# Leaving out the dummy matmuls at the norm borders of a four-layer transformer kernel on one NeuronCore

## The chip, the cores and the metric

The kernel runs on one NeuronCore of a Trainium2 chip. The metric is the device time of one execution in microseconds (us). The kernel before takes 1987.98 us, the median of three runs (1987.39 to 1991.22).

TensorE (PE) does the matmuls, VectorE (DVE), ScalarE (ACT) and GpSimd (POOL) the element-wise work; SyncE (SP) issues most DMAs. PE's rows in the trace are of two kinds, PE for the matmul itself and PEld for the load of its stationary operand.

## The reference

Two blocks in a row on x of 512 tokens by 1024 features, in float32. The first has two layers (an HGRN2 and stick-breaking mixer, then an mLSTM mixer, each followed by a convolutional gated feed-forward net), the second has one (dilated and sparse attention, then a gated feed-forward net). Every mixer and every feed-forward net is fed by the same kind of step, an RMS norm with a gain and a shift that come from a conditioning vector:

```python
def rmsnorm(x, g):
    xf = x.astype(jnp.float32)
    y = xf * lax.rsqrt(jnp.mean(xf * xf, axis=-1, keepdims=True) + EPS)
    return y * g.astype(jnp.float32)

def modulate(x, g, shift, scale):
    return (rmsnorm(x, g) * (1.0 + scale) + shift).astype(x.dtype)
...
        h = modulate(x, norm_mix_g[layer], sh_m, sc_m)
        ...
        x = x + (g_m * y).astype(x.dtype)
        h = modulate(x, norm_ffn_g[layer], sh_f, sc_f)
        x = x + (g_f * conv_glu_ffn(h, ffn_w_in[layer], ffn_conv_w[layer], ffn_conv_b[layer],
                                    ffn_w_out[layer])).astype(x.dtype)
```

The output projection of one stage must be finished before the mean square over the features is known, and that must be known before the first matmul of the next projection.

## The kernel before

Features lie on the partitions, tokens along the free axis, so the residual stream x is 8 tiles (KT) of 128 by 512. Weights are streamed from memory by SP in chunks of 128 x 1024 (`w_raw`); POOL splits each chunk into a high and a low part (`w_hi`, `w_lo`), once PE has let go of the buffers, and each product is three matmuls, high by high, high by low, low by high (L447 to L449 in `three`; L474 to L476 where the tokens are the stationary side). Results go to four banks called `gemm`. A projection chunk is 24 such matmuls.

The order on each engine is the order in which its program is written; engines meet at semaphores. There is no scheduler.

A **norm border** is the place between the last projection of a stage and the first of the next. There are six, numbered r: 1 (`even_out` to `ffn0`), 2 (`down0` to `odd_in`), 3 (`odd_out` to `ffn1`), 4 (`down1` to `idx_in`), 5 (`attn_out` to `ffn2`), 6 (`down2` to the final norm and the output). At a border the engines do in turn:

1. PE sums the squares of the first seven tiles over the features, which DVE has collected in `sq_acc`: four one-column matmuls (L536, `partial_sums` in `norm_scale`).
2. DVE adds the last projection tile to `x_res`, ACT squares it (`sq_tile`, L1724), and PE adds that to the sum (L536 again). At border 4 two norms come in a row, and PE sums 8 more for the second (`work`).
3. ACT takes the root (`rms`, L1729 or L2046), DVE the reciprocal (`rstd`, L1114; at border 4 further small steps down to L1147).
4. PE spreads `rstd` over all partitions, with four matmuls against the identity matrix (L558, `bcast`).
5. DVE scales (L1151), ACT shifts and rounds to the high part (`h_hi`, L1738), DVE subtracts for the low part (`h_lo`, L1158), tile by tile; PE starts the next projection with the first tile (`first_tiles`, which takes two output tiles at a time and waits at each of the eight k for `h_lo`).

Between these steps PE is given matmuls whose result nobody reads. They go to bank `M[0]` and are issued by one helper:

```python
            def keep_warm(n):

                for _ in range(n):
                    pe.matmul(M[0][:, 0:256], const("ones"), cst[:, 0:256], start=True, stop=True)
```

With `WARM = (2, 4, 4, 14)` each of borders 1, 2, 3 and 5 has 2 of them between steps 1 and 2, 1 after step 2 and 4 after step 4; border 4 has 2, 3 and 4; border 6 has 2, 1 and none. Four more stand after the first norm at the start of the kernel. That is 4 + 4 x 7 + 9 + 3 = 44. The 14 at the very start (`WARM[3]`) are a loop of their own.

A float32 matmul shows as two instructions in the trace, so one dummy is two records of 128 x 256 on L531, and a spread of four matmuls is eight records on L558.

Of the kernel before, what the change touches and what calls it, by code (L numbers as in the profile page):

```python
# [73 lines left out]
    _g = tuple(a + b for a, b in zip(_g, _u))  # L74
ADA_EARLY = 16
ADA_SLOTS = 4
WARM = (2, 4, 4, 14)

DOWN = (8, 8, 6)

# [90 lines left out]
def build(nc, x_in, wstream, adastream, c_in, cols_in, const_in, mask_in, gatew_in, wuk_in, wuv_in, out):  # L171
    with ExitStack() as ctx:
# [3 lines left out]
        def sb(name, shape, dt=F32, where=ctx):  # L176
            return where.enter_context(nc.sbuf_tensor(name, shape, dt))
# [12 lines left out]
        cst = sb("cst", [P, CST["dist"]])  # L190
# [8 lines left out]
        M = [ctx.enter_context(nc.psum_tensor(f"mix{i}", [P, T], F32)) for i in range(4)]  # L199
# [3 lines left out]
        def const(name, n=128, rows=P):  # L203
            return cst[0:rows, CST[name]:CST[name] + n]
# [136 lines left out]
        def sig(name):  # L341

            if name not in S:
                S[name] = sem(name)
            return S[name]
# [99 lines left out]
        def _(pe):  # L445
# [79 lines left out]
                            mm.then_inc(pe_done, 1)  # L525
                            c += 1

            def keep_warm(n):

                for _ in range(n):  # L530
                    pe.matmul(M[0][:, 0:256], const("ones"), cst[:, 0:256], start=True, stop=True)  # L531

            def partial_sums(c0, tile, first, last):

                for j in range(NTB):
                    mm = pe.matmul(normps[:, c0 + j:c0 + j + 1], tile[:, j * P:(j + 1) * P], const("ones")[:, 0:1],  # L536
                                   start=first and j == 0, stop=last, skip_group_check=True)
                return mm

            def norm_scale(r):  # L540

                pe.wait_ge(sq_added, KT * r + KT - 1)
                partial_sums(0, sqacc, True, False)
                keep_warm(WARM[0])
                pe.wait_ge(sq_ready, KT * (r + 1))
                mm = partial_sums(0, sqt[:, 1, :], False, True)
                if r == 4:
                    pe.wait_ge(gsq_added, KT)
                    partial_sums(4, work[:, 2, :], False, False)
                    pe.wait_ge(gsq_ready, KT)  # L550
                    mm = partial_sums(4, work[:, 1, :], False, True)
                mm.then_inc(norm_sum, 1)
                keep_warm(3 if r == 4 else 1)

            def token_rows(ps, c0):

# [5 lines left out]
            def bcast(ps, count, c0=0):  # L562
                pe.wait_ge(rstd_ready, count)
                token_rows(ps, c0).then_inc(rstd_bc, 1)
# [3 lines left out]
            def norm(r):  # L568
                norm_scale(r)
                bc[0] += 1  # L570
                bcast(rstdps, bc[0])
                if r not in (0, 6):
                    keep_warm(WARM[2])


            pe.wait_ge(sig("ones_set"), 1)
            for _ in range(WARM[3]):
                pe.matmul(M[0][:, 0:256], sqacc[:, 0:P], sqacc[:, 0:256], start=True, stop=True)
            pe.wait_ge(sq_added, KT - 1)
            for j in range(NTB):  # L580
# [2 lines left out]
            pe.wait_ge(const_in_sem, 16)  # L583
            bc[0] += 1
            bcast(rstdps, bc[0])
            keep_warm(WARM[2])

            def stick_z(h):
                if h == 0:
# [162 lines left out]
            pe.wait_ge(h_ready, KT * FILL["even_out"] + 7)  # L752
            tiles("even_out", 2)
            norm(1)
            tiles("ffn0", 11)
            down("down0", 0)
            norm(2)

            tiles("odd_in", 2)
# [147 lines left out]
            for u in range(4):  # L907
                tile_chunk(4 + N0["odd_out"] + u, (N0["odd_out"] + u) % SPL, u, 1 + G0["odd_out"][u])
            norm(3)
            tiles("ffn1", 11)  # L910
            down("down1", 1)

            norm_scale(4)
            bc[0] += 1
            bcast(rstdps, bc[0] + 1, 8)
            keep_warm(WARM[2])

            first_tiles("idx_in", FILL["idx_in"])

# [1324 lines left out]
```

## Time and profile before

| | |
|---|---|
| median of three runs | 1987.98 us (1987.39 to 1991.22) |
| the profiled execution, its own time | 1991.48 us |
| its span (first to last instruction) | 1989.7 us |
| outside the span | 1.8 us |
| mean granted TensorE clock over the span | 0.985 |
| PE busy | 1923.1 us, 97% |
| share of the chain that ended last, PE | 86% |
| dummy matmuls at borders and after the first norm | 44 (88 records) |

All times of the rows below are of the one profiled execution. Its own time is 3.5 us above the median of the runs. The clock is given as a share of full speed: 1.00 is 2.4 GHz, 0.50 is 1.2 GHz. A stretch that holds both levels shows a mean. Matmuls are pipelined, so the duration of one row is longer than its step to the next; what one costs in a stream is the distance of two starts.

### The profile page before, as it was taken

What the parts mean: (1) busy time and instruction counts of PE and PEld (TensorE: products, weight loads), DVE (VectorE), ACT (ScalarE), POOL (GpSimd) and SP (SyncE); (2) the same over time, 40 slices, a digit from 0 to 9 for tenths busy, and PEclk for the clock granted to TensorE, in tenths of its full rate; (3) what the DMA queues carried; (4) which work ended last, traced back from release to release, by engine and by line L of the source; (5) the groups of instructions that cost most, each with busy time, mean ns of one, the idle gap of its engine ahead of it and who ended that gap; (6) DMA issues with size and microseconds to landing.
All of it is one profiled execution on the core that took longest, in us unless ns stands there. A gap on an engine that the chain in (4) does not pass through costs nothing.

```text
span 1989.7 us, 25330 instructions
## 1 busy us (share of the span) xinstructions
PE 1923.1 (97%) x8824; PEld 1551.2 (78%) x8824; DVE 1034.7 (52%) x1529; ACT 451.9 (23%) x774; POOL 1184.4 (60%) x907
## 2 busy tenths in 40 slices
PE   5999999999999999999999999999988899999998
PEld 4787868888888887667788888887766688888886
DVE  7566256666655453466766663233877453323222
ACT  3302342211210022352221211112228421111100
POOL 3743326788887955324688787746540256666773
PEclk7999999999999999999999999999989999999999
DMA  7432223455554422111455553322210023222332
GB/s 305 177 117 75 96 95 106 170 190 192 204 193 174 172 96 85 53 52 55 157 191 193 197 189 117 105 96 85 74 59 17 27 82 104 95 95 95 106 105 74
DMA packets 67375, 242.23 MB, mean 122 GB/s; under 512 B 7498, under 2 KB 7882, under 8 KB 67314
## 3 DMA queue, kind: packets, MB, share of 16 engines
q1 hardware_dynamic: 65536, 237.01, 34.2%
q10 hardware_dynamic: 1778, 4.37, 0.6%
q8 instruction: 43, 0.70, 0.1%
q14 instruction: 18, 0.15, 0.0%
HBM read 239.25 MB, written 2.10 MB: 121 GB/s over the span
## 4 chain that ended last, share of the span: by engine, by line
PE 86%; DVE 7%; ACT 3%; issue 2%; DMA 2%; POOL 1%; DVEq 0%; SPq 0%; ACTq 0%; POOLq 0%
PE gemm L447 23%; PE gemm L448 23%; PE gemm L449 23%; DMA w_raw<-wstream 2%; DVE b_score L1630 1%; PE mix L650 1%; PE gemm L474 1%; PE gemm L476 1%; PE gemm L475 1%; DVE b_top L1625 1%; PE mix L447 1%; PE gemm L1046 1%; PE gemm L803 1%; DVE sq_acc L1365 1%; PE mix L449 1%
## 5 line engine op out<-in xcount | busy, mean ns | idle before, releaser
L431 POOL TENSOR_TENSOR w_lo<-w_raw,w_hi 128x1024 fp32r<-128x1024 f32 x302 | 734.9, 2433 | 25.2
L447 PE MATMUL gemm<-h_hi,w_hi 128*128 128x512 f32 x1616 | 634.0, 392 | 20.8 <-DVE h_lo L1186 14.6
L448 PE MATMUL gemm<-h_lo,w_hi 128*128 128x512 f32 x1616 | 630.1, 390 | 0.0
L449 PE MATMUL gemm<-h_hi,w_lo 128*128 128x512 f32 x1616 | 630.1, 390 | 0.0
L428 POOL TENSOR_TENSOR pool_gate<-pool_gate 128x1 f32<-128x1 f32 x298 | 118.3, 397 | 734.4 <-PE gemm L449 592.8
L447 PEld LDWEIGHTS gemm<-h_hi,w_hi 128*128 128x128 f32 x1616 | 304.2, 188 | 90.2 <-issue 21.8
L429 POOL TENSOR_SCALAR w_hi<-w_raw 128x1024 fp32r<-128x1024 f32 x302 | 344.1, 1139 | 17.5 <-DMA w_raw<-wstream 17.5
L449 PEld LDWEIGHTS gemm<-h_hi,w_lo 128*128 128x128 f32 x1616 | 304.0, 188 | 63.8
L448 PEld LDWEIGHTS gemm<-h_lo,w_hi 128*128 128x128 f32 x1616 | 304.1, 188 | 62.0
L1080 DVE CUSTOM_DVE_ANT_0 ada_raw<-ada_raw,c_act 128x1024 f32<-128x1024 f32 x128 | 216.5, 1707 | 110.1 <-DMA ada_raw<-adastream 110.1
L449 PE MATMUL gemm<-p_hi,w_lo 128*128 128x512 f32 x528 | 205.4, 389 | 0.0
L447 PE MATMUL gemm<-p_hi,w_hi 128*128 128x512 f32 x528 | 205.4, 389 | 0.0
L448 PE MATMUL gemm<-p_lo,w_hi 128*128 128x512 f32 x528 | 205.4, 389 | 0.0
L1098 DVE SCALAR_TENSOR_TENSOR x_res<-gemm,modv,x_res 128x512 f32<-128x512 f32 x48 | 35.9, 747 | 238.7 <-PE gemm L449 238.7
L1393 DVE TENSOR_TENSOR work<-work,gemm 128x512 f32<-128x512 f32 x66 | 45.4, 688 | 176.5 <-PE gemm L449 140.3
L1395 DVE TENSOR_TENSOR p_lo<-work,p_hi 128x512 f32 x66 | 98.6, 1494 | 61.4 <-ACT p_hi L1927 61.4
L1724 ACT ACTIVATE sq_tile<-x_res 128x512 f32 x48 | 30.3, 632 | 430.4 <-DVE x_res L1098 430.4
L1365 DVE TENSOR_TENSOR sq_acc<-sq_acc,sq_tile 128x512 f32<-128x512 f32 x42 | 98.6, 2348 | 36.7 <-ACT sq_tile L1724 36.7
L449 PEld LDWEIGHTS gemm<-p_hi,w_lo 128*128 128x128 f32 x528 | 99.1, 188 | 20.8
L448 PEld LDWEIGHTS gemm<-p_lo,w_hi 128*128 128x128 f32 x528 | 99.1, 188 | 20.6
L447 PEld LDWEIGHTS gemm<-p_hi,w_hi 128*128 128x128 f32 x528 | 99.1, 188 | 20.4
L1921 ACT ACTIVATE work<-work 128x512 f32<-128x512 f32 x44 | 27.8, 633 | 307.1 <-DVE work L1388 307.1
(339 smaller groups left out, 1972.0 us busy)
## 6 DMA issues: line engine op xcount, KB each, us to landing
w_raw<-wstream SPq DMA_DIRECT2D x302, 512.0 KB, 3.5
ada_raw<-adastream SPq DMA_DIRECT2D x128, 512.0 KB, 4.3
a_early<-adastream SPq DMA_DIRECT2D x8, 1024.0 KB, 11.9
out<-x_res SPq DMA_DIRECT2D x8, 256.0 KB, 2.2
c_act<-c_in ACTq DMA_DIRECT2D x2, 512.0 KB, 7.2
x_res<-x_in SPq DMA_DIRECT2D x2, 512.0 KB, 6.3
x_res<-x_in ACTq DMA_DIRECT2D x2, 512.0 KB, 9.0
b_dist<-const_in ACTq DMA_DIRECT2D x1, 512.0 KB
```

The lines of the kernel that those rows point to most:

```text
L428: pool.tensor_tensor(pgate[:], pgate[:], pgate[:], ALU.mult)
L429: pool.tensor_scalar(whi[s][:], raw[:, u % RAW, :], 1.0, 0.0, ALU.mult, ALU.add).then_inc(w_hi_done, 1)
L431: pool.tensor_tensor(wlo[s][:], raw[:, u % RAW, :], whi[s][:].bitcast(F32), ALU.subtract).then_inc(w_split, 1)
L447: pe.matmul(out_ap, w_h, r_h, start=first, stop=False)
L448: pe.matmul(out_ap, w_h, r_l, start=False, stop=False)
L449: return pe.matmul(out_ap, w_l, r_h, start=False, stop=last)
L1080: dve.tensor_tensor_reduce(w, w, c, 1.0, start, ALU.mult, ALU.add, total).then_inc(ada_used, 1)
L1098: dve.scalar_tensor_tensor(out=X[:, ds(m, 1), :].rearrange("p a t -> p (a t)"), in0=G[bank][:], scalar=modv[:, ds(gate + m, 1)], in1=X[:, ...
L1365: dve.tensor_tensor(sqacc[:], sqacc[:], sqt[:, m % 2, :], ALU.add).then_inc(sq_added, 1)
L1393: dve.tensor_tensor(work[:, 2 + jj, :], y, G[2 * jj + 1][:], ALU.mult).then_inc(gfree[2 * jj + 1], 1)
L1395: dve.tensor_tensor(Plo[:, ds(2 * i + jj, 1), :].rearrange("p a t -> p (a t)"), work[:, 2 + jj, :], Phi[:, ds(2 * i + jj, 1), :].rearrange ...
L1724: act.activation(sqt[:, slot, :], X[:, ds(m, 1), :].rearrange("p a t -> p (a t)"), ACT.Square).then_inc(sq_ready, 1)
```

## The change

All calls of `keep_warm` go, and the helper with them. The 14 matmuls at the very start stay. Nothing else is changed, and no wait is added or moved. The diff, whole but for the last place, which is like the others:

```diff
-WARM = (2, 4, 4, 14)
+WARM = 14
...
-            def keep_warm(n):
-
-                for _ in range(n):
-                    pe.matmul(M[0][:, 0:256], const("ones"), cst[:, 0:256], start=True, stop=True)
-
...
                 pe.wait_ge(sq_added, KT * r + KT - 1)
                 partial_sums(0, sqacc, True, False)
-                keep_warm(WARM[0])
                 pe.wait_ge(sq_ready, KT * (r + 1))
                 mm = partial_sums(0, sqt[:, 1, :], False, True)
...
                 mm.then_inc(norm_sum, 1)
-                keep_warm(3 if r == 4 else 1)
...
                 norm_scale(r)
                 bc[0] += 1
                 bcast(rstdps, bc[0])
-                if r not in (0, 6):
-                    keep_warm(WARM[2])
...
-            for _ in range(WARM[3]):
+            for _ in range(WARM):
                 pe.matmul(M[0][:, 0:256], sqacc[:, 0:P], sqacc[:, 0:256], start=True, stop=True)
...
             bcast(rstdps, bc[0])
-            keep_warm(WARM[2])
```

PE's instructions at border 1 before; `mix` is the group of banks that sums, spread and dummies are written to:

```order
L536 MATMUL mix<-cst,sq_acc 128x1 x4
L531 MATMUL mix<-cst 128x256 x2
L536 MATMUL mix<-cst,sq_tile 128x1 x4
L531 MATMUL mix<-cst 128x256
L558 MATMUL mix<-cst,rstd 128x128 x4
L531 MATMUL mix<-cst 128x256 x4
L447 MATMUL gemm<-h_hi,w_hi 128x512
```

And after the change, where the line numbers are smaller by 5 (sums) and 7 (spread):

```order
L531 MATMUL mix<-cst,sq_acc 128x1 x4
L531 MATMUL mix<-cst,sq_tile 128x1 x4
L551 MATMUL mix<-cst,rstd 128x128 x4
L447 MATMUL gemm<-h_hi,w_hi 128x512
```

The three groups of dummies are gone, and what is left stands in the same order.

PE's instructions at border 4 before:

```order
L536 MATMUL mix<-cst,sq_acc 128x1 x4
L531 MATMUL mix<-cst 128x256 x2
L536 MATMUL mix<-cst,sq_tile 128x1 x4
L536 MATMUL mix<-cst,work 128x1 x8
L531 MATMUL mix<-cst 128x256 x3
L558 MATMUL mix<-cst,rstd 128x128 x4
L531 MATMUL mix<-cst 128x256 x4
```

And after:

```order
L531 MATMUL mix<-cst,sq_acc 128x1 x4
L531 MATMUL mix<-cst,sq_tile 128x1 x4
L531 MATMUL mix<-cst,work 128x1 x8
L551 MATMUL mix<-cst,rstd 128x128 x4
```

Nine matmuls are gone there, and the sums are followed at once by the spread.

## Rows read from the trace of the kernel before

**Rows 1.** The page: busy time by engine, the chain's shares, POOL's wait per chunk.

```profile
PE 1923.1 (97%) x8824; PEld 1551.2 (78%) x8824; DVE 1034.7 (52%) x1529; ACT 451.9 (23%) x774; POOL 1184.4 (60%) x907
...
PE 86%; DVE 7%; ACT 3%; issue 2%; DMA 2%; POOL 1%; DVEq 0%; SPq 0%; ACTq 0%; POOLq 0%
...
L428 POOL TENSOR_TENSOR pool_gate<-pool_gate 128x1 f32<-128x1 f32 x298 | 118.3, 397 | 734.4 <-PE gemm L449 592.8
```

**Rows 2.** Border 1, PE in order of time: start, duration, name, idle before.

```profile
335.63 0.39 PE L448 MATMUL gemm<-h_lo,w_hi 128*128 128x512 f32 x1
...
336.09 0.95 PE L536 MATMUL mix<-cst,sq_acc 128*128 128x1 f32 x8
336.90 1.11 PE L531 MATMUL mix<-cst 128*128 128x256 f32 x4
337.93 1.05 PE L536 MATMUL mix<-cst,sq_tile 128*128 128x1 f32 x8
338.85 0.68 PE L531 MATMUL mix<-cst 128*128 128x256 f32 x2
339.62 1.16 PE L558 MATMUL mix<-cst,rstd 128*128 128x128 f32 x8
340.61 1.89 PE L531 MATMUL mix<-cst 128*128 128x256 f32 x8
343.39 0.47 PE L447 MATMUL gemm<-h_hi,w_hi 128*128 128x512 f32 x1 [0.88 <-DVE h_lo L1158]
```

**Rows 3.** Border 1, ACT and DVE in order of time.

```profile
337.25 0.63 ACT L1724 ACTIVATE sq_tile<-x_res 128x512 f32 x1 [4.82 <-DVE x_res L1098]
...
339.39 0.18 DVE L1114 RECIPROCAL rstd<-rms 128x4 f32<-128x4 f32 x1 [1.77 <-ACT rms L1729]
...
342.35 0.75 DVE L1158 SCALAR_TENSOR_TENSOR h_lo<-work,modv,h_hi 128x512 fp32r<-128x512 f32 x1
...
343.68 0.74 DVE L1158 SCALAR_TENSOR_TENSOR h_lo<-work,modv,h_hi 128x512 fp32r<-128x512 f32 x1
```

**Rows 4.** Border 4, PE and DVE in order of time.

```profile
1324.99 2.91 PE L531 MATMUL mix<-cst 128*128 128x256 f32 x6
1327.69 1.91 PE L558 MATMUL mix<-cst,rstd 128*128 128x128 f32 x8
1329.40 2.62 PE L531 MATMUL mix<-cst 128*128 128x256 f32 x8
1332.19 0.47 PE L447 MATMUL gemm<-h_hi,w_hi 128*128 128x512 f32 x1 [0.17 <-issue]
...
1326.88 0.17 DVE L1147 TENSOR_TENSOR rstd<-rstd 128x4 f32<-128x4 f32 x1
```

**Rows 5.** Stretches: length, PE busy (records), granted clock, DMA share, GB/s.

```profile
23.60:26.90 3.30, 0.00 (x0) 1.00 1.03 410
35.60:40.60 5.00, 4.99 (x12) 0.50 0.83 329
187.40:190.80 3.40, 1.14 (x5) 1.00 0.49 151
190.80:194.20 3.40, 3.40 (x9) 0.50 0.13 27
1320.00:1324.00 4.00, 4.00 (x33) 1.00 0.61 167
1324.00:1330.80 6.80, 6.80 (x25) 0.50 0.60 211
1330.80:1334.20 3.40, 3.23 (x15) 0.99 0.03 7
```

**Rows 6.** The dummies after the first norm and the first projection, PE.

```profile
19.38 3.62 PE L531 MATMUL mix<-cst 128*128 128x256 f32 x8
...
36.17 0.63 PE L448 MATMUL gemm<-h_lo,w_hi 128*128 128x512 f32 x1
36.60 0.63 PE L449 MATMUL gemm<-h_hi,w_lo 128*128 128x512 f32 x1
```

More of the change, by code:

```diff
@@ L915, in _ @@
             bcast(rstdps, bc[0] + 1, 8)
-            keep_warm(WARM[2])
             first_tiles("idx_in", FILL["idx_in"])
```

## Prediction

> **What bounds the kernel now.** I read the page first: PE is busy 97% of the span and holds 86% of the chain that ended last [rows 1], so a microsecond lost on PE outside a wait is a microsecond of the kernel, unless PE waits later for something that the loss does not delay. Nothing catches up later: POOL's splitting of the weights waits for PE, 592.8 us in all before its gate instruction [rows 1], not the other way, so there is no backlog that PE could work off faster once it has lost time. The mean granted clock is 0.985, so the clock is a thing that this kernel now mostly has, and can lose. Then I read border 1 in order of time, PE against DVE and ACT, to see what each dummy stands in front of [rows 2, 3], the same at border 4, which is longer [rows 4], and last the granted clock of stretches around each place where it fell [rows 5].
>
> **What the dummies cost today.** At border 1 two stand before the second sum. The square that this sum waits for ends at 337.25 + 0.63 = 337.88, and the sum starts at 337.93 [rows 2, 3]; they cost nothing. One stands before the spread: `rstd` is ready at 339.39 + 0.18 = 339.57 and the spread starts at 339.62. Nothing. Four stand before the next projection, and PE then idles 0.88 us for `h_lo` (342.35 + 0.75 = 343.10, start 343.39) [rows 2, 3]. Nothing again. Borders 2, 3 and 5 have the same steps. At border 4 the three dummies before the spread do cost something: `rstd` is ready at 1326.88 + 0.17 = 1327.05 and the spread starts at 1327.69 [rows 4]. Without them it would start 0.05 us after `rstd`, as at border 1, so the change gains 0.6 us there. That is all there is to gain with certainty: **0.6 us**.
>
> **What the dummies give today.** They keep PE at work between 336.09 and 343.39. Left without them at border 1 are sums of one column each, eight records of spread that take 339.62 to 340.61 = 1.0 us, and waiting, 7.3 us in all [rows 2]. What does the clock do in such a stretch? The nearest row is border 4 itself: from 1320.00 to 1324.00 PE has 33 records, four of them dummies and nearly all the others one-column sums, and at 1324.0 the granted clock falls to 0.50 (1.2 GHz), where it stays until 1330.8 [rows 5]. So it falls even with two dummies among the sums, within 4.0 us of the last projection matmul. A second row: from 187.4 to 190.8 PE is busy 1.14 us, and at 190.8 the clock falls for 3.4 us. A third: the four dummies at the start end at 19.38 + 3.62 = 23.0 [rows 6], PE is idle after them, the clock is still 1.00 from 23.6 to 26.9 and 0.50 when the projection starts [rows 5]. In the changed kernel each border has 7.3 us whose only full-width work is 1.0 us of spread, no more than stood before any of these falls. I expect the clock to fall at all five borders that a projection follows (1 to 5).
>
> The Trainium skill speaks against this step. Its page "TensorE: Matmul & The Clock Gate", section "HAM oscillation — how this bites in real kernels", gives the rule as one on idle gaps: the clock falls when PE idles for longer than a limit. The longest idle piece of the changed border 1 would be from the end of the spread to 343.39, and that is within the page's limit, so by that rule the clock would hold and the time would be that of the first rival below. The row from 1320.00 to 1324.00 speaks against the rule as worded: PE busy 4.00 of 4.00 us, and yet a fall.
>
> **The cost of a restart at the low level.** At 1.00 one projection matmul follows the next in 335.86 - 335.63 = 0.23 us [rows 2]; at 0.50 in 36.60 - 36.17 = 0.43 us [rows 6]. While the clock is low PE loses 1 - 0.23/0.43 = 0.47 us per us. Does a wait cover it? In the first tiles PE needs 6 matmuls per k, 6 x 0.23 = 1.38 us, and DVE gives an `h_lo` each 343.68 - 342.35 = 1.33 us [rows 3]. PE is already the slower one by 0.05 us; at 0.43 it needs 2.6 us per k, so nothing covers the loss. How long does the low level last once projection matmuls run? The row that is most like it is the first projection: it starts after an idle stretch and is low from 35.6 to 40.6, 5.0 us. Two other low stretches with PE busy throughout are 3.4 us (from 190.8) and 6.8 us (from 1324.0) [rows 5]. I take 5.0 us, the row most like it, and 3.4 and 6.8 as bounds. Per border 5.0 x 0.47 = 2.35 us (1.6 to 3.2). Border 4 pays it too: today its low stretch is spent on sums, dummies and spread, and the projection starts at 0.99 [rows 4, 5]; without dummies it starts low. **Five borders: 11.8 us** (8.0 to 16.0).
>
> **The cost of a spread at the low level.** Low, a spread takes 1329.40 - 1327.69 = 1.7 us [rows 4], at full clock 340.61 - 339.62 = 1.0 us [rows 2], and DVE waits for it: +0.7 us, with up to 0.3 more if the last sum before it is low as well. Border 4 pays that today already. At borders 1, 2, 3, 5 and 6 the spread starts 3.5 us after the last projection matmul and the fall came 4.0 us after it at border 4; without the dummies it comes sometimes sooner. I take half of 0.8 for each of the five: **2.0 us** (0 to 5).
>
> **The start.** Before the first projection PE idles from 23.0 to 35.6 and the clock is low at 35.6 with the dummies there [rows 5, 6]. Without them it is low as well: **0**. The dummies there end long before `h_lo`, so nothing is gained either. **Border 6** is followed by no projection: only its spread counts, above.
>
> **The sum.** 11.8 + 2.0 - 0.6 = +13.2 us. Against the profiled execution's own time 1991.5 + 13.2 = 2004.7; that execution is 3.5 us above the median, so against the median 1987.98 + 13.2 = 2001.2, rounded to **2001 us**. The bounds of the terms give 1987.98 + 8.0 - 0.6 = 1995.4 and 1987.98 + 16.0 + 5.0 - 0.6 = 2008.4.
>
> **The rivals.**
>
> *The clock holds.* If the spread in the middle of the border is enough for the clock to stay at 1.00 at borders 1, 2, 3 and 5, and border 4 falls as before, all that is left is the 0.6 us gained and one restart of 2.35: 1989.7, no change. If border 4 holds as well, 1987.4. For it: the longest idle piece is short (end of spread to 343.39), and the clock stayed at 1.00 for 3.3 us of full idleness from 23.6 to 26.9. Against it: the falls at 190.8 and 1324.0 came with PE doing more than it will here. 4%.
>
> *The dummies were in the way, and the kernel gets faster.* The mechanism: dummies already issued hold up the real matmul behind them. Border 4 shows 0.6 us, and each first projection matmul starts 0.29 us after its `h_lo` (343.10 to 343.39) where a spread answers in 0.05. If all of this went at five borders with the clock kept, the gain is 0.6 + 5 x 0.25 = 1.8 us, and with the spread at border 4 at full clock 0.7 more: 1985.5. It decides only if the clock never falls there. To be over 0.2% (4 us) faster it would have to bring more than the trace shows anywhere: 2%.
>
> *The clock falls at some borders only.* Where the fall comes relative to the border may differ from one to the next, and the clock may be back before the projection starts. With two of five: 2 x 2.35 + 1.0 - 0.6 = +5.1, 1993.1. For it: the clock stayed at 1.00 from 23.6 to 26.9 with PE idle throughout [rows 5], so a fall is not instant. Against: all five stretches are alike and 7 us or more. 9%.
>
> *The low level lasts longer.* Each restart 6.8 us, each spread and last sum low: 5 x 3.2 + 5 x 1.0 - 0.6 = +20.4, 2008.4; beyond it if the delays push other thin stretches (stick-breaking, mLSTM, attention) into falls of their own, 1.6 us each. 12%.
>
> **How the numbers follow.** Forecast 73%, longer 12%, some only 9%, clock holds 4%, faster 2%. What the measurement can tell from no change is about 0.2%, 4 us, 1984 to 1992. Faster 2%. Same: the clock that holds, and a part of the "some only" case: 5%. Slower: 93%. The range runs from 1994.5, just under the lower bound of the terms, to 2008.4, their upper one; it leaves out most of the "some only" case and the far end of the longer one.
>
> **What would show it.** Right: the clock at 0.50 when the first projection matmul of `ffn0`, `odd_in`, `ffn1`, `idx_in` and `ffn2` starts, their rows at steps of 0.43 for some 5 us; the mean clock down from 0.985 to about 0.975 (five to six borders with some 7 us more at 0.50 each, 40 x 0.5 / 2003 = 0.010); the gap from the last projection matmul to the next unchanged at 7.3 us where the spread is at full clock, about 8.1 where it is low. Border 4: spread 0.05 us after `rstd`, projection some 0.6 us sooner than the 12.2 us of today, but low. PE's records fewer by 88, its busy time not lower by as much as the dummies took. Wrong: clock at 1.00 through the borders, which takes the whole forecast with it; or a loss at the borders and a shorter wait later, for which I see no place in a chain that is 86% PE.

## The result and the profile after

The kernel without the dummies takes 2004.09 us, the median of four runs (2003.13 to 2004.24), against 1989.60 us before in the same comparison (four runs, 1987.39 to 1991.40). The ratio is 1.0071, 95% interval 1.0059 to 1.0083: slower by 14.5 us. The forecast was 2001 us, within 1994.5 to 2008.4.

The page of the kernel after, busy time and the clock in 40 slices:

```profile
PE 1914.0 (96%) x8736; PEld 1545.1 (77%) x8736; DVE 1030.2 (51%) x1529; ACT 451.8 (23%) x774; POOL 1179.9 (59%) x907
...
PEclk7999998999999989999999999989989989999998
```

PE has 88 records fewer than in [rows 1], as it should, and is busy 9.1 us less, though the dummies' records covered 26.8 us: the projections took back most of it, since a record at the low clock lasts longer (0.63 us against 0.39). The mean granted clock is 0.972, against 0.985. The span is 2002.4 us, 12.7 more than before; this is the time in the profile that has to be found.

Border 1 of the kernel after, PE in order of time (start, duration, name, idle before). It answers to [rows 2]:

```profile
334.69 0.95 PE L531 MATMUL mix<-cst,sq_acc 128*128 128x1 f32 x8
336.53 1.05 PE L531 MATMUL mix<-cst,sq_tile 128*128 128x1 f32 x8 [0.89 <-ACT sq_tile L1713]
338.22 1.86 PE L551 MATMUL mix<-cst,rstd 128*128 128x128 f32 x8 [0.64 <-DVE rstd L1103]
342.67 0.76 PE L447 MATMUL gemm<-h_hi,w_hi 128*128 128x512 f32 x1 [2.58 <-DVE h_lo L1147]
343.23 0.63 PE L448 MATMUL gemm<-h_lo,w_hi 128*128 128x512 f32 x1
```

The order is the old one without L531's dummies (that line number now belongs to the sums). The spread starts 3.53 us after the first sum, as before; it lasts 1.86 us instead of 1.16; and the projection's matmuls last 0.63 us each, as they do at the start of the kernel before [rows 6], where the clock is low.

The same kernel by stretches (length, PE busy and records, granted clock, DMA share, GB/s). The first four rows are border 1; then come the first projection matmuls behind borders 2, 3, 4 and 5:

```profile
334.70:338.40 3.70, 2.17 (x18) 1.00 0.66 261
338.50:342.60 4.10, 1.58 (x8) 0.50 0.63 236
342.70:348.70 6.00, 6.00 (x14) 0.50 0.03 13
348.80:352.00 3.20, 3.20 (x16) 1.00 0.00 0
713.20:717.40 4.20, 4.20 (x10) 0.50 0.01 4
966.10:969.90 3.80, 3.80 (x9) 0.50 0.14 56
1338.40:1342.00 3.60, 3.60 (x9) 0.50 0.01 2
1626.60:1632.10 5.50, 5.50 (x13) 0.50 0.00 0
```

All five restarts are at 0.50, for 6.1, 4.3, 3.9, 3.7 and 5.6 us, read from start to the clock's return (the stretches above are cut a little inside these).

To weigh a border by itself I take, for each, the time from its first column sum to its first projection matmul (the gap), and to the 49th projection matmul, when the eight k of the first two tiles are done (at border 4 to the spread that stands right behind the 48th). Both are differences of two starts in the trace:

| border | gap before | gap after | to 49th before | to 49th after | cost |
|---|---|---|---|---|---|
| 1 | 7.30 | 7.97 | 18.31 | 21.80 | +3.49 |
| 2 | 7.27 | 8.46 | 18.25 | 21.41 | +3.16 |
| 3 | 7.18 | 7.02 | 18.17 | 19.86 | +1.69 |
| 4 | 12.19 | 11.29 | 23.19 | 23.99 | +0.80 |
| 5 | 7.27 | 8.18 | 18.27 | 21.77 | +3.50 |
| 6, from the first sum to the end of the span | | | 12.64 | 14.09 | +1.45 |

The sum is +14.09 us. Ahead of border 1 the kernel after is 1.40 us earlier (first sum at 334.69 against 336.09): a fall of the clock at 190.8 that the profile of before has [rows 5] is not in this one (`190.80:194.20` is at 1.00 there). 14.09 - 1.40 = 12.69, the 12.7 us of the spans.

### The profile page after: what moved, and what is told of

Its sections match the earlier page's. It is cut to its first block, busy times and chain, and to the rows that moved or that the text cites. A ratio compares the mean times of both kernels' runs of the same rounds, so it can differ in the third digit from the quotient of the medians.

```text
span 2002.4 us, 25154 instructions
## 1 busy us (share of the span) xinstructions
PE 1914.0 (96%) x8736; PEld 1545.1 (77%) x8736; DVE 1030.2 (51%) x1529; ACT 451.8 (23%) x774; POOL 1179.9 (59%) x907
## 4 chain that ended last, share of the span: by engine, by line
PE 85%; DVE 7%; ACT 3%; issue 2%; DMA 2%; POOL 1%; DVEq 0%; ACTq 0%; SPq 0%; POOLq 0%
PE gemm L447 23%; PE gemm L449 23%; PE gemm L448 23%; DMA w_raw<-wstream 2%; DVE b_score L1619 1%; PE mix L640 1%; PE gemm L474 1%; PE gemm L476 1%; PE gemm L475 1%; DVE b_top L1614 1%; PE gemm L793 1%; PE gemm L1035 1%; PE mix L447 1%; DVE sq_acc L1354 1%; PE mix L448 1%
## 5 line engine op out<-in xcount | busy, mean ns | idle before, releaser
L428 POOL TENSOR_TENSOR pool_gate<-pool_gate 128x1 f32<-128x1 f32 x298 | 110.8, 372 | 750.4 <-PE gemm L449 609.4
```

Of the source, the lines that this page charges most:

```text
L428: pool.tensor_tensor(pgate[:], pgate[:], pgate[:], ALU.mult)
```

## The experiments

My theory: the clock falls in the thin stretch of each border because PE has too little wide matmul work there, and each fall is paid where PE is the bound, in the first projection matmuls and in the spread. The rivals: PE's idle pieces as such let the clock fall; only the idle piece ahead of the projection matters; a restart costs the same wherever it is; and, on the side of the dummies, that they cost PE time of their own.

### One-column dummies: is it idle time or is it work?

```diff
-                for _ in range(n):
-                    pe.matmul(M[0][:, 0:256], const("ones"), cst[:, 0:256], start=True, stop=True)
+                for _ in range(2 * n):
+                    pe.matmul(M[0][:, 0:1], const("ones"), cst[:, 0:1], start=True, stop=True)
```

> Every dummy at the borders and after the first norm becomes two one-column matmuls (columns 0 to 1 instead of 0 to 256), which at full clock keep PE in work, weight loads included, for about as long as the one wide dummy did (4 x 0.11 = 0.45 us against 0.43). Theory (what holds the clock is the streamed work of the dummies, not that PE is never idle): the clock falls to 0.50 at all five borders, each restart of the projection is low for 3.4 to 6.8 us, and the time is that of the kernel after the change, 2004, or some microseconds more, since at the low clock the eight one-column matmuls behind the spread last 16 x 0.21 = 3.4 us and can end after the first h_lo: 2004 to 2010 us. Rival (an idle piece lets the clock fall): PE has as little idle time as in the kernel before, the clock stays at 1.00 at borders 1, 2, 3 and 5, and the time is 1988 to 1991 us.

Measured: 2004.7 us (2004.33 to 2006.2), ratio 1.0077 (1.0060 to 1.0094), about as with no dummies at all (1.0071). Border 1 by stretches:

```profile
336.10:340.70 4.60, 4.41 (x39) 1.00 0.54 207
340.80:343.60 2.80, 2.80 (x15) 0.50 0.85 281
343.70:347.60 3.90, 3.90 (x10) 0.50 0.15 60
```

PE is busy 4.41 of 4.60 us, with matmuls and with loads of full 128 x 128 stationary tiles, and at 340.8 the clock falls all the same; it falls at all five borders that a projection follows. So PE kept busy by one-column matmuls does not hold the clock, and PE kept busy for the same time by the wide ones of the kernel before does: what holds the clock here is the width of the dummies, not that they leave no idle piece. How wide they must be was not tested; only 1 and 256 columns were. The rule of the Trainium skill's page "TensorE: Matmul & The Clock Gate", section "HAM oscillation — how this bites in real kernels", which is worded by idle gaps, would have the clock hold here; the measurement decides against that wording. The idle-gap rival falls. That the total is that of the kernel after is in part a coincidence: at the low level the sixteen narrow matmuls behind the spread last 3.24 us at border 1 and delay the projection (gap 7.62 us, against 7.30 before), while the restart is shorter, 3.9 us against 6.1.

### Which dummies carry it

Only the four behind the spread kept (both calls in `norm_scale` taken out):

```diff
-                keep_warm(WARM[0])
...
-                keep_warm(3 if r == 4 else 1)
```

> Only the dummies behind the spread stay (four at each of borders 1 to 5 and four after the first norm); those ahead of it (2 and 1, at border 4 2 and 3, at border 6 2 and 1) go. Theory: the stretch of sums and waiting from the last projection matmul to the spread, 3.5 us, is thin again, so the clock falls at some of the borders, ahead of or during the dummies behind the spread; but those are wide and run low for a while, so it is back at 1.00 at or soon after the first projection matmul. Per border 0 to 2 us, mean 0.8, plus up to 1 us at border 6: 1989 + 4 = 1993 us (1990 to 1998). Rival (only the long idle piece in front of the projection matters): all loss is avoided, 1989 us. Rival (every dummy counts alike): four of seven stay, so three sevenths of the 14.5 us are lost, 1996 us.

Measured: 1995.7 us over seven runs (1992.97 to 2000.93), ratio 1.0030 (1.0018 to 1.0041). Border 3, PE in order of time:

```profile
960.44 1.73 PE L536 MATMUL mix<-cst,sq_tile 128*128 128x1 f32 x8 [0.44 <-ACT sq_tile L1722]
962.81 2.07 PE L556 MATMUL mix<-cst,rstd 128*128 128x128 f32 x8 [0.64 <-DVE rstd L1112]
964.67 3.27 PE L531 MATMUL mix<-cst 128*128 128x256 f32 x8
967.59 0.58 PE L447 MATMUL gemm<-h_hi,w_hi 128*128 128x512 f32 x1
```

And the same border by stretches:

```profile
960.70:967.40 6.70, 6.07 (x23) 0.50 0.73 271
967.50:971.00 3.50, 3.50 (x17) 1.00 0.00 0
```

The clock had fallen by the second sum (1.73 us instead of 1.05); spread and dummies ran low, and it was back when the first projection matmul started. That border has a gap of 8.64 us instead of 7.18, but a restart at full clock: +1.56 to the 49th. Border 2 held (+0.02), borders 1, 4 and 5 cost 0.62, 1.02 and 1.84, and border 6 cost 1.06. The time is higher than my 1993 and inside its range. The second rival's 1996 (every dummy alike) fits the total at least as well; against it stand only the borders, which go from nothing to 1.8, in one profile, and that is of the slowest of the seven executions (2000.93 us). It is not ruled out as a rule for the mean.

Only those ahead of the spread kept (the three `keep_warm(WARM[2])` taken out):

```diff
-                if r not in (0, 6):
-                    keep_warm(WARM[2])
```

> Only the dummies ahead of the spread stay (2 and 1 at borders 1, 2, 3, 5, 6; 2 and 3 at border 4); the four behind the spread go at every border and after the first norm. Theory: the spread runs at full clock at borders 1, 2, 3 and 5, as before (1.0 us), the gap to the first projection matmul stays 7.3 us, but the thin stretch behind the spread, 2.8 us idle, lets the clock fall at some borders, now around or after the first projection matmul: 0 to 3 us each, mean 1.2, border 4 1.6, total 1989 + 6.5 = 1996 us (1992 to 2001). Rival (only the long idle piece in front of the projection matters): the whole loss of the change bar the spreads comes back, 2001 to 2002 us.

Measured: 1995.3 us over nine runs (1993.52 to 1998.12), ratio 1.0034 (1.0023 to 1.0044), near the 1996 of the theory and far from the 2001 of the rival. Border 1 by stretches:

```profile
336.00:343.20 7.20, 4.59 (x31) 1.00 0.63 232
343.30:346.70 3.40, 3.40 (x8) 0.50 0.25 99
```

Here the spread is at full clock and the gap is 7.27 us. The fall comes at 343.3, when the idle stretch is over and the projection is just starting. At border 2 of the same trace three projection matmuls start at full clock before it, the first at 711.32:

```profile
711.30:711.90 0.60, 0.58 (x3) 1.00 0.12 48
712.00:715.30 3.30, 3.30 (x10) 0.50 0.00 0
```

**The clock lags what PE did.** It costs 1.6 us at each of borders 1, 2 and 3, 0.7 at border 4 and nothing at border 5. The two halves of the dummies save different things, the first half the spread and the start of the restart, the second half the restart; neither half alone saves both.

### One border alone

The dummies were taken out at border 1 and nowhere else (`r == 1` added to the conditions in `norm_scale` and `norm`).

> The dummies go at border 1 alone and stay everywhere else. Theory: the clock falls at border 1 alone; from the last projection matmul before it to the 49th after it takes 18.3 + 1.9 to 3.5 us = 20.2 to 21.8 us, the later borders read as before (18.2 to 18.3 us each, border 4 22 to 24), so what a border costs does not depend on what was done at the others; total 1989 + 2.9 = 1992 us. Rival (a fall at one border shifts or multiplies falls at later ones): borders 2, 3 or 5 show low restarts too.

Stretches: border 1, its restart, then borders 2, 3 and 5.

```profile
334.60:342.00 7.40, 3.39 (x25) 0.79 0.63 243
342.10:345.70 3.60, 3.60 (x9) 0.50 0.15 59
703.00:710.20 7.20, 6.26 (x39) 1.00 0.61 192
955.70:962.80 7.10, 6.16 (x38) 1.00 0.79 271
1610.00:1617.20 7.20, 6.30 (x39) 1.00 0.40 145
```

To the 49th matmul border 1 takes 20.19 us (+1.9), the others 18.25, 18.17 and 18.27 as before. Border 4, low before and after, has a gap of 12.79 us instead of 12.19. So at borders 2, 3 and 5 nothing of the fall at border 1 is seen, and the forecast may be added up border by border. But a border's cost is not one number: up to here the program is that of the kernel after but for the four dummies at the start, and border 1 costs 1.9 us in this execution and 3.5 in that one. The whole execution, 1990.9 us and the only one, is no measure of 1.9 us: falls outside the borders came and went by as much.

### Border 4 alone

```diff
-                keep_warm(WARM[0])
+                keep_warm(0 if r == 4 else WARM[0])
...
-                keep_warm(3 if r == 4 else 1)
+                keep_warm(0 if r == 4 else 1)
...
             bcast(rstdps, bc[0] + 1, 8)
-            keep_warm(WARM[2])
```

> The dummies go at border 4 alone. There the clock falls with them as well, so they cost 0.6 us of delay before the spread and save a low restart. Theory: the gap from the last projection matmul to the first of idx_in shrinks by 0.6 to 0.9 us (12.2 to 11.3 to 11.6), the restart is low for 3.4 to 6.8 us and costs 1.6 to 3.2, net +0.7 to +2.6 us: 1991 us (1989 to 1993). Rival (at border 4 the dummies are only in the way): 1988 to 1989 us, and a restart at full clock.

Measured: 1992.33 us over ten runs, against 1989.75 before, ratio 1.0018 (1.0009 to 1.0028). PE at border 4 in order of time:

```profile
1320.88 2.97 PE L536 MATMUL mix<-cst,work 128*128 128x1 f32 x16
1325.81 2.07 PE L558 MATMUL mix<-cst,rstd 128*128 128x128 f32 x8 [1.96 <-DVE rstd L1146]
1330.49 0.77 PE L447 MATMUL gemm<-h_hi,w_hi 128*128 128x512 f32 x1 [2.62 <-DVE h_lo L1157]
```

And its restart as a stretch, low for 4.7 us:

```profile
1330.50:1335.20 4.70, 4.70 (x11) 0.50 0.02 5
```

The 49th matmul comes 25.54 us after the first sum, +2.35 against the low border of before. The 0.6 us of delay before the spread is gone, as forecast, but the gap did not shrink (12.37 us): the clock fell during the sums, which took 2.97 us instead of 2.39. "Only in the way" is refuted, by the interval of the ratio and by the restart: the dummies are worth more at border 4 than they cost.

### The start: a low restart that costs nothing

```diff
             bcast(rstdps, bc[0])
-            keep_warm(WARM[2])
+            keep_warm(30)
```

> Thirty dummies instead of four after the first norm, so that PE comes warm to the first projection. Theory: the first projection matmuls run at 1.00, steps of 0.23 instead of 0.43, but the first matmul still starts at 35.6 to 35.9, when its h_lo is there, and the following tiles wait for theirs (the kernel before idles 0.43, 0.78 and 0.79 us for h_lo at 46.8, 50.6 and 54.4), so the low restart of the start was hidden and the 25th w_hi matmul from there on starts at the same time: 0 gained. Rival (a low restart costs 2.3 us wherever it is): everything from 60 us on is 2.3 us earlier.

PE in order of time at the start:

```profile
19.41 14.62 PE L531 MATMUL mix<-cst 128*128 128x256 f32 x60
35.57 0.47 PE L447 MATMUL gemm<-h_hi,w_hi 128*128 128x512 f32 x1 [1.54 <-DVE h_lo L1186]
...
39.18 0.50 PE L447 MATMUL gemm<-h_hi,w_hi 128*128 128x512 f32 x1 [0.61 <-DVE h_lo L1186]
...
42.99 0.50 PE L447 MATMUL gemm<-h_hi,w_hi 128*128 128x512 f32 x1 [0.79 <-DVE h_lo L1186]
```

And the first 5 us of the projection as a stretch:

```profile
35.60:40.60 5.00, 4.39 (x18) 1.00 0.82 328
```

The restart is now at 1.00, against 0.50 in [rows 5], and it gains nothing: PE waits 0.61 and 0.79 us for each next `h_lo`, which comes every 3.8 us, and the 49th `w_hi` matmul starts 0.1 us from where it did. At the start 12 matmuls per k share a feed of 3.8 us: 12 x 0.23 = 2.8 us of work at full clock, 12 x 0.43 = 5.2 at half. The low restart of the kernel before makes PE late for a tile or two, and the waits for the next tiles at full clock take the delay back. At a border 6 matmuls share a feed of 1.33 us, which is less than their 1.38 at full clock, so there is no slack to take anything back. A low clock costs only where PE at full clock would not have waited anyway, as at borders 1 to 5.

### More dummies than the cover holds

```diff
-WARM = (2, 4, 4, 14)
+WARM = (2, 4, 8, 14)
```

> Eight dummies instead of four behind the spread at borders 1 to 5 and after the first norm. The idle piece in front of the projection at full clock is 0.88 us, which covers two of the four added, 0.43 us each; the other 0.87 us delays the projection. Theory (dummies cost nothing as long as they end ahead of h_lo, and their full time beyond it): the gap at borders 1, 2, 3 and 5 goes from 7.3 to 8.1 us, at border 4, where nothing is idle, by 1.7 us, total +5 us, 1994.5 us. Rival (PE takes dummies in its stride, the projection does not wait for them): 1989.6 us.

Measured: 1993.88 us over ten runs, ratio 1.0023 (1.0013 to 1.0032). PE at border 1:

```profile
338.81 3.62 PE L531 MATMUL mix<-cst 128*128 128x256 f32 x16
342.08 0.58 PE L447 MATMUL gemm<-h_hi,w_hi 128*128 128x512 f32 x1
```

The gap is 7.79 us instead of 7.27 to 7.30: four more dummies, 1.72 us, delay its first matmul by 0.5, at each of borders 1, 2, 3 and 5; at border 4, which held its clock in this profile, the gap is 10.89 us against 10.38 where it held with four, in the profile of the filled start, 0.5 again instead of the 1.7 forecast. To the 49th matmul the delay is 0.6 at each (18.89 us against 18.31 at border 1), since the first record starts right behind the last dummy and lasts 0.58 instead of 0.47. Five borders make 3 us; the medians differ by 4.1 and the ratio allows 2.6 to 6.4, so the total agrees and cannot tell this from the theory's 5. The cover is then 1.72 - 0.6 = 1.1 us, not the 0.88 that the row of before states as idle: that figure is counted from the modelled end of the last dummy, its start plus 0.38 us, while the next may start after 0.22, and 0.88 + 0.16 = 1.04. Four dummies cost nothing here; eight do.

### Can border 4 be made shorter with real work?

The four sums of the second norm that wait for nothing were moved ahead of the two dummies, with 30 dummies at the start as above:

```diff
                 partial_sums(0, sqacc, True, False)
+                if r == 4:
+                    pe.wait_ge(gsq_added, KT)
+                    partial_sums(4, work[:, 2, :], False, False)
                 keep_warm(WARM[0])
...
                 if r == 4:
-                    pe.wait_ge(gsq_added, KT)
-                    partial_sums(4, work[:, 2, :], False, False)
...
-            keep_warm(WARM[2])
+            keep_warm(30)
```

> All dummies stay; at border 4 the four column sums of the first seven tiles of the second norm, which wait for nothing, are issued ahead of the two dummies instead of behind the sum that waits for the last square; thirty dummies instead of four after the first norm. Theory: the chain at border 4 is shorter by the four sums, 8 x 0.11 to 8 x 0.21 = 0.9 to 1.7 us, unless the delay is taken by the gain's last square (0.71 us behind the first): the gap from the last projection matmul to the first of idx_in goes from 12.2 to about 11.2 us, and the time to 1988.5 us against 1989.6. Rival (the clock falls earlier, since the thin stretch ahead of the spread is as long): no change.

Measured: 1991.11 us over ten runs, ratio 1.0005 (0.9996 to 1.0015), no change. In its profile and in that of the filled start border 4 happened to hold its clock; the gaps are 10.22 and 10.38 us. The move gained 0.16 us of the 0.9 forecast, because the two dummies now ended behind the square and stood in the way of its sum. So the next kernel left out those two at border 4 (`keep_warm(0 if r == 4 else WARM[0])`), had four instead of three ahead of the spread, and the start as before:

> The kernel before with one border changed: at border 4 the four sums of the second norm that wait for nothing take the place of the two dummies ahead of the last square, and four dummies instead of three stand ahead of the spread. In the kernel with the gain sums first the two dummies behind them ended 0.86 us after the last square was ready (1325.42 against 1324.56), so the moved sums gained only 0.17 us. Theory (real work in the place of dummies shortens the chain, and clock is lost only if what is left is too thin): where border 4 holds its clock the gap is 10.4 - 0.9 = 9.5 us, and 48 matmuls on 20.5 us instead of 21.4; but the stretch of sums is now without any dummy, so the clock falls in more executions, and then the gap is 11.5 to 12.2. Time 1988 to 1991 us against 1989.7, same within what can be told. Rival (two dummies there do not matter for the clock): 0.9 us faster.

Measured: 1986.90 us over twelve runs against 1990.38, ratio 0.9991 (0.9983 to 1.0000). In its profile border 4 was low for 3.4 us instead of 6.8 and took 21.65 us to the 49th matmul instead of 23.19. That is not the moved sums alone: with the old order and its clock held, in the profile of the filled start, border 4 took 21.37 us. It was run once more, unchanged:

> The kernel with the sums in the place of two dummies at border 4, once more and unchanged, since its interval just touched no change (0.9983 to 1.0000). Theory: the gain at border 4 is real, 1.5 us to the 49th projection matmul in its profile, and its times are two groups, about 1986.5 and about 1991 to 1993, by which falls an execution has: median 1986.5 to 1989, ratio 0.9985 to 0.9998. Rival (the first median was a favourable draw of falls elsewhere): ratio 1.000 and the two medians within 0.5 us.

Measured: 1988.49 us against 1990.64, ratio 0.9994 (0.9985 to 1.0003). Both are lower, by 3.5 and 2.2 us at the medians and 1.8 and 1.2 by the ratios, and neither is clear of no change. It is not shown that this version beats the kernel before; if there is a gain it is about 0.1%.

### The same programs once more

> The kernel after the change once more, unchanged, for a second profile. Theory (the clock falls at every border, and only how long it stays low once the projection runs changes from one execution to the next): 0.50 at the first projection matmul of all five borders again, low for between 3.4 and 6.8 us there, each border's length another than in the first profile, sum within 3 us of the first; 2001 to 2006 us. Rival (the length of the low restart belongs to the border): the same five lengths as in the first profile, 6.1, 4.3, 3.9, 3.7 and 5.6 us.

The kernel after took 2008.58 us in this one execution, above what I had expected. Its restarts by stretches, borders 1 to 5:

```profile
344.20:349.90 5.70, 5.70 (x14) 0.50 0.01 5
714.60:718.60 4.00, 4.00 (x10) 0.50 0.01 4
969.80:974.60 4.80, 4.80 (x12) 0.50 0.01 3
1342.50:1346.60 4.10, 4.10 (x10) 0.50 0.01 2
1631.00:1636.80 5.80, 5.80 (x14) 0.50 0.00 0
```

Low at all five again, 24.5 us of restarts against 23.4. Four of the five lengths are within 0.5 us of the first profile's; border 3 is another (4.8 against 3.9) and its spread is low this time, and it costs 2.94 us instead of 1.69. So neither side of this test is clean: the lengths vary, but less than the bounds of 3.4 to 6.8 allow. The other microseconds are outside the borders: this execution has the fall at 189.5, as the kernel before has it, and another at 913 that neither of the first two profiles has, 3.4 us low each and so about 1.6 us.

> The kernel before once more, unchanged, for a second profile. Theory: borders 1, 2, 3 and 5 at 1.00 throughout and 18.2 to 18.3 us each to the 49th projection matmul, as in the first profile; border 4 either low (12.2 to 12.8 us to the first projection matmul, 23 us to the 49th) or at full clock (10.4 and 21.4), as two of the kernels that keep the dummies have shown; the falls at 190, 808, 1454, 1471 and 1556 us at other places or absent, and the time anywhere in 1986.5 to 1991.6 us. Rival (with the same program the falls are the same): border 4 low, and every fall where it was.

The kernel before took 1991.28 us, and its falls were where they had been, border 4 low with a gap of 12.23 us:

```profile
1319.90:1323.70 3.80, 3.80 (x32) 1.00 0.64 175
1323.90:1330.50 6.60, 6.60 (x23) 0.50 0.59 215
```

In this pair the rival was right. That the falls can differ is shown by other kernels. In the one with only the dummies behind the spread, whose program is that of the kernel before up to border 1, the clock falls at 134.6, with the same 6.04 us of PE work in the 6.8 us ahead of it:

```profile
127.70:134.50 6.80, 6.04 (x38) 1.00 0.33 135
134.60:141.40 6.80, 6.80 (x23) 0.50 0.45 154
```

and in the kernel before it does not:

```profile
127.70:134.50 6.80, 6.04 (x39) 1.00 0.33 130
134.60:141.40 6.80, 6.68 (x35) 1.00 0.44 154
```

That fall cost 2.8 us. The clock thus falls in a thin stretch in some executions and not in others. Over the 70 executions of the kernel before that ran beside the experiments, the time follows the mean granted clock: 1986.5 to 1987.2 us in the three at 0.988, 1993.3 to 1993.4 in the three at 0.984. The low level is half of full speed, so a mean lower by 0.004 is some 0.008 x 1990 = 16 us more at the low level, by estimate 16 x 0.47 = 7.5 us, and the two groups are 6.5 apart. So most of the spread between equal kernels goes with the time that the clock was low. What decides where the clock falls I did not test.

## Why the prediction was right, point by point

**The bound, and that nothing catches up.** Right. Behind each border the difference between the kernels stays what it was at the 49th matmul until the next one; from border 1 to border 2, for one, +2.1 us over all of `ffn0`.

**What the dummies cost.** At borders 1, 2 and 5 nothing, as said: the kernel after has the same 3.53 us to the spread at border 1. At border 3 the prediction took the steps to be those of border 1, and they are not. There the first sum itself waits for `sq_acc`, the two dummies start late, and the second sum starts 0.42 us after its square (ready at 955.11); without them it starts 0.05 after (ready at 960.46):

```profile
955.53 0.95 PE L536 MATMUL mix<-cst,sq_tile 128*128 128x1 f32 x8
...
960.51 1.05 PE L531 MATMUL mix<-cst,sq_tile 128*128 128x1 f32 x8 [0.45 <-ACT sq_tile L1713]
```

The first row is of the kernel before, the second of the kernel after. The spread comes 3.18 us after the first sum instead of 3.44, so the dummies cost 0.26 us there, which the forecast lacks. At border 4 the spread started at 1333.67, 0.05 us after `rstd` (1333.46 + 0.16), with the gap 0.90 us shorter; forecast 0.6. The rest of the 0.9 is the clock, which in that profile fell behind the sums and not within them (1.93 us for `work` instead of 2.39).

**The clock falls at all five.** Right in both profiles, and the one-column dummies show why it was right to go by the row at border 4, with PE busy throughout, and not by idle pieces. One row of the prediction was misread, though. The clock was not "still" 1.00 from 23.6 to 26.9. The four dummies at the start ran low (3.62 us, against 1.89 at border 1), and the clock rose only when they were over:

```profile
13.40:23.50 10.10, 7.32 (x24) 0.50 1.03 408
```

So the clock came up 0.6 us after PE had gone idle, and was not held over from the dummies' own time. The forecast does not rest on this; the rival with some borders only drew on it, and what holds of that is that the clock stayed at 1.00 for 3.3 us with PE idle.

**The restart.** Forecast 5.0 us each at a loss of 0.47 us per us, 11.8 us in all. Measured lengths 6.1, 4.3, 3.9, 3.7 and 5.6, mean 4.7, so 23.4 x 0.47 = 11.0 us. The rate is borne out border by border: growth of the gap plus length x 0.47 gives each cost of the table to 0.05 us. The length of 5.0 was borrowed from the start, a place with another history, and there is luck in its fit: single restarts went from 3.6 us (border 1 alone) to 6.1.

**The spread at the low level.** Forecast 0.4 per border, 2.0 in all with 0 to 5 as bounds. Measured as the growth of the gap at 1, 2, 3 and 5, 0.67 + 1.19 - 0.16 + 0.91 = 2.6, and 1.45 at border 6, together 4.1 us. This term was undersized by half: I had the fall come 4.0 us after the last projection matmul, as at border 4 today, but without the two dummies ahead of the second sum it came 3.8, 2.5, 3.5 and 2.2 us after it at borders 1, 2, 5 and 6, in time for the spread (only border 3, with 4.1, kept a fast one), and at border 6 for the second sum as well. PE there, in order of time:

```profile
1990.17 1.56 PE L531 MATMUL mix<-cst,sq_tile 128*128 128x1 f32 x8 [0.89 <-ACT sq_tile L1713]
...
1992.30 2.08 PE L551 MATMUL mix<-cst,rstd 128*128 128x128 f32 x8 [0.56 <-DVE rstd L1103]
```

**The start.** Forecast nothing; +0.3 us in one profile, 0.1 in the other. Right, and for a second reason that the prediction did not give: even a restart at full clock gains nothing there.

**The sum.** 11.0 + 4.1 - 0.9 = 14.2 us at the borders (14.1 by the table), forecast 13.2; the comparison of runs says 14.5. That the sum is this close is partly errors of opposite sign: 0.8 too much for the restarts and 0.3 too little gained at border 4, against 2.1 too little for the spreads. The median of before in that comparison was 1989.6 and not 1988.0, which is the other part of why 2001 was 3 us low.

## What to carry to other kernels

Where PE is the bound on both sides of a serial stretch, look at the width of what it runs in that stretch and not only at how long it idles: wide dummies that end within a wait that is there anyway are free, and the 44 here keep 14.5 us; one-column ones kept nothing. Read each border for itself: the same two dummies were free at border 1 and cost 0.26 us at border 3. Count their cover from starts, not from the modelled ends, and put them on both sides of any short piece of real work. Before filling a stretch, check that PE is the slower side behind it; if it waits for its feed, the clock is worth nothing there.

## What the runs showed of the hardware that I had not expected

The clock can fall when the thin stretch is already over, in the first projection matmuls (343.3 and 712.0, with the dummies ahead of the spread only), and cost 1.6 us there. One-column matmuls with full weight loads, PE busy 4.41 of 4.60 us, did not hold it. And the same 6.04 us of work in 6.8 us at the same place was followed by a fall in one execution and not in another.
